# A gate projection by Strassen-Winograd's seven half-block products, beside a state space stage and a prompt attention stage

## The reference

```python
u = rms_norm(x, lp['norm_g'][0])
nq, nkv, ngate, sz, sxbc, sdt, dqkv, mg = split_in(u @ lp['w_in'])
...                                   # o_a, o_b, o_cc: the three mixers
gates = jax.nn.sigmoid(mg.reshape(B, T, 3, D_MODEL).astype(jnp.float32)).astype(x.dtype)
mix = (gates[:, :, 0] * o_a + gates[:, :, 1] * o_b + gates[:, :, 2] * o_cc) @ lp['w_out']
```

```python
cb = jnp.einsum('bcihn,bcjhn->bcijh', Cc, Bc) * decay * dtc[:, :, None]
y_diag = jnp.einsum('bcijh,bcjhp->bcihp', cb, xc)
h_last, h_in = lax.scan(step, h0.astype(f32), (jnp.moveaxis(states, 1, 0), jnp.moveaxis(chunk_decay, 1, 0)))
y_off = jnp.einsum('bcihn,bchpn,bcih->bcihp', Cc, h_in, jnp.exp(acum))
```

## Time and profile before

| | |
|---|---|
| median of 3 runs | 3345.62 us (3342.29 to 3346.05) |
| the profiled execution | 3336.09 us |
| its span in the trace | 3334.3 us |
| mean granted TensorE clock | 0.951 of full |
| PE busy | 3026.4 us (91%) |
| DVE busy | 1254.0 us (38%) |
| ACT busy | 640.2 us (19%) |
| POOL busy | 468.8 us (14%) |

### The profile page before, as it was taken

One profiled execution on the slowest core, in us unless ns is written; L12 is line 12 of the kernel. 1 busy time (PEld: TensorE's weight loads), 2 busy tenths in 40 slices (PEclk: granted clock), 3 DMA queues, 4 the chain that ended last, 5 costly groups with the idle time before them and its releaser, 6 DMA issues. The chain is left out here.

```text
span 3334.3 us, 42907 instructions
## 1 busy us (share of the span) xinstructions
PE 3026.4 (91%) x15198; PEld 2011.2 (60%) x15198; DVE 1254.0 (38%) x2964; ACT 640.2 (19%) x1528; POOL 468.8 (14%) x351
## 2 busy tenths in 40 slices
PE   7999989798998888798999889799689999998998
PEld 5777766565555555445545556355478888873443
DVE  2111123233641666154554344123355655560000
ACT  2111000001321233133333221134301111110000
POOL 0001000003310433100000000011123223320000
PEclk8999999899998889899999989799899999999999
DMA  7545252426962532621110242401033433404000
GB/s 160 132 89 98 81 151 87 132 83 178 278 198 88 169 111 63 192 70 37 31 40 33 98 153 92 174 13 38 26 134 109 150 109 118 140 24 164 33 33 25
DMA packets 336639, 344.79 MB, mean 103 GB/s; under 512 B 60945, under 2 KB 305361, under 8 KB 335078
## 3 DMA queue, kind: packets, MB, share of 16 engines
q1 hardware_dynamic: 298074, 265.85, 27.4%
q10 hardware_dynamic: 38390, 76.67, 6.8%
HBM read 289.11 MB, written 110.01 MB: 120 GB/s over the span
## 5 line engine op out<-in xcount | busy, mean ns | idle before, releaser
L284 PE MATMUL d_ps<-d_w,mixer_u_T 128*128 128x288 f32 (+2 forms) x2048 | 618.8, 442 | 22.3 <-DVE d_ob L308 15.8
L284 PEld LDWEIGHTS d_ps<-d_w,mixer_u_T 128*128 128x128 f32 x2048 | 380.3, 197 | 160.1 <-issue 45.1
L288 PE MATMUL d_ps<-mixer_u_T,d_w 128*128 128x352 f32 x1152 | 426.9, 496 | 12.3 <-PEq L145 9.7
L2883 PE MATMUL down_ps<-down_w,feed_g_T 128*128 128x512 f32 x704 | 305.2, 596 | 10.6 <-DMA down_w<-ffn_w_down 10.6
L288 PEld LDWEIGHTS d_ps<-mixer_u_T,d_w 128*128 128x128 f32 x1152 | 205.4, 198 | 118.0 <-issue 55.1
L2883 PEld LDWEIGHTS down_ps<-down_w,feed_g_T 128*128 128x128 f32 x704 | 134.5, 191 | 179.7 <-issue 168.4
L3097 PE MATMUL ffn_ps<-up_u_T,ffn_w 128*128 128x264 f32 x704 | 164.6, 393 | 0.7 <-DVE ffn_taps L3243 0.7
L308 DVE COPY d_ob<-d_ps 128x288 f32<-128x288 f32 (+3 forms) x144 | 66.3, 462 | 261.9 <-PE d_ps L284 167.8
L3097 PE MATMUL ffn_ps<-ffn_T,ffn_w 128*128 128x264 f32 x704 | 163.8, 386 | 0.0
L3097 PE MATMUL ffn_ps<-up_u_T,ffn_S 128*128 128x264 f32 x704 | 163.8, 386 | 0.0
L3097 PEld LDWEIGHTS ffn_ps<-up_u_T,ffn_w 128*128 128x128 f32 x704 | 133.4, 192 | 23.5 <-issue 0.9
(11 more groups left out here) (464 smaller groups left out, 3788.4 us busy)
## 6 DMA issues: line engine op xcount, KB each, us to landing
out_dil_sample<-cache_dil_w ACTq DMA_DIRECT2D x10, 3264.0 KB
ffn_w<-ffn_w_up SPq DMA_DIRECT2D x44, 512.0 KB, 4.9
cmp_rows<-cache_nsa_kv SPq DMA_DIRECT2D x128, 128.0 KB
graw<-d_ob SPq DMA_DIRECT2D x72, 176.0 KB
mix_gate<-graw SPq DMA_DIRECT2D x24, 528.0 KB, 6.1
dils_qb<-proj SPq DMA_DIRECT2D x24, 512.0 KB, 7.0
d_w<-w_in SPq DMA_DIRECT2D x24, 512.0 KB, 5.3
ssd_x<-proj SPq DMA_DIRECT2D x29, 384.0 KB, 4.8
```

Of the source, the lines that this page charges most:

```text
L284: mm = pe.matmul(self.ps[u % 2][0:rows, 0:cols], self.u_T[:, k, r0:r0 + rows], self.view(i)[:, k, :], start=(k == 0), stop=(k == DK - 1))
L288: mm = pe.matmul(self.ps[u % 2][:, 0:cols], self.view(i)[:, k, x, :], self.u_T[:, k, c * third:(c + 1) * third], start=(k == 0), stop=(k = ...
L2883: mm = pe.matmul(ps[i % ring][:, 512 * h:512 * (h + 1)], lhs_T[:, k, r0:r0 + m], w[:, k, 512 * h:512 * (h + 1)], start=(k == 0), stop=(k = ...
```

## The change

The gate projection leaves `Dense` for a class of its own, `Gates`. It takes the weights in pairs of blocks (A, 2 by 2 half blocks: two rows of 128 channels, two columns of 512 features) and the activations in halves (B: two of 512 features, two of 528 tokens), and computes the four half blocks of the product by seven products instead of eight. Each of the seven runs twice, for x = 0 and 1, over 264 tokens, with 4 steps: 14 products and 56 steps for a pair, 6 pairs a stage, so 336 steps and 672 PE instructions of 264 columns a stage where there were 288 and 576 of 352. P1 is copied out by ACT to `kept`; every other result is taken out of PSUM by a DVE addition with what was kept (14 of 128x264 a pair, 84 a stage; two of them behind P5). A bank is used by the products of one x in turn, so a product waits until the addition before it on that bank is done. The sums S of weights (4 a pair, 128x512) are GpSimd's, the sums T of activations are made once by DVE at the head of the `ssd` stage. The stores to `graw` become 96 of 128x264 in place of 72 of 128x352.

To make room, `oa` in `nsap` has two heads' places instead of four, so that ACT waits for a store before it writes a place again; and in `ssd` two small buffers are laid over others (`junk` over `yout`, `last_rows` over `skip`) with a wait on ACT each.

```diff
+class Gates:
+    ORDER = [(p, x) for p in ("P1", "P2", "P6", "P7", "P5", "P4", "P3") for x in range(2)]
+    OUTS = [("C11", 0), ("C11", 1), ("C22", 0), ("C22", 1), ("C21", 0), ("C21", 1), ("C12", 0), ("C12", 1)]
...
+        last_reader = dict(P6="C11", P7="U", P5="W", P4="V", P3="C21")
+        operands = dict(P1=(lambda i: self.A(i, 0, 0), lambda x: self.B(0, 0, x)),
+                        P2=(lambda i: self.A(i, 0, 1), lambda x: self.B(1, 0, x)),
+                        P6=(lambda i: self.S(2), lambda x: self.T_of(1, x)),
+                        P7=(lambda i: self.S(3), lambda x: self.B(0, 1, x)),
+                        P5=(lambda i: self.A(i, 1, 0), lambda x: self.T_of(0, x)),
+                        P4=(lambda i: self.A(i, 1, 1), lambda x: self.T_of(2, x)),
+                        P3=(lambda i: self.S(4), lambda x: self.B(1, 1, x)))
...
+                for p, x in ORDER:
+                    if p == "P2":
+                        pe.wait_ge(self.held, 2 * i + x + 1)
+                    elif p != "P1":
+                        pe.wait_ge(self.summed, self.added(i, last_reader[p], x))
+                    elif i:
+                        pe.wait_ge(self.summed, self.added(i - 1, "C12", x))
...
+                    for k in range(KH):
+                        mm = pe.matmul(self.ps[x][:, 0:self.quarter], lhs(i)[:, k, :], rhs(x)[:, k, :], start=(k == 0), stop=(k == KH - 1))
...
+                        act.copy(self.kept[:, 0, x, :], self.ps[x][:, 0:self.quarter]).then_inc(self.held, 1)
...
+            def add(i, name, x, base, out):
+                if (name, x) in OUTS:
+                    o = OUTS.index((name, x))
+                    n = len(OUTS) * i + o
+                    if n >= RING:
+                        dve.wait_ge(self.stored[o % RING], 16 * (n // RING))
+                    out = self.ob[:, o % RING, 0:self.quarter]
+                dve.tensor_tensor(out, base, self.ps[x][:, 0:self.quarter], ALU.add).then_inc(self.summed, 1)
...
+                    if p == "P2":
+                        add(i, "C11", x, first, None)
+                    elif p == "P6":
+                        add(i, "U", x, first, second)
+                    elif p == "P7":
+                        add(i, "W", x, second, first)
+                    elif p == "P5":
+                        add(i, "C22", x, first, None)
+                        add(i, "V", x, second, second)
+                    elif p == "P4":
+                        add(i, "C21", x, first, None)
+                    elif p == "P3":
+                        add(i, "C12", x, second, None)
...
+                pool.tensor_tensor(self.S(3), self.A(i, 0, 0), self.A(i, 1, 0), ALU.subtract).then_inc(self.S_made, 1)
...
+        return Lane(KH * NP * pairs, pe_program, act_program, dve_program, pool_program, sp_program)
...
-    oa = st.sb("oa", [P, NSA_R, SEQ])
+    oa = st.sb("oa", [P, 2, SEQ])
...
-            act.activation(junk[0:m, :], y[0:m, :], ACT.Square, accum_out=ss[0:m, 0:1]).then_inc(squared, 1)
+            if n >= 2:
+                act.wait_ge(stored[slot], s_count(n, slot))
+            act.activation(yout[0:m, slot, :], y[0:m, :], ACT.Square, accum_out=ss[0:m, 0:1]).then_inc(squared, 1)
...
-            ssd(nc, ins, outs, proj, y_b, ident, [(dense.lane(36, settle=False), 0, 1)])
+                ssd(nc, ins, outs, proj, y_b, ident, [(gates_of.lane(6), 0, 1)])
...
-                together(nc, (dense.lane(36), 0, 1), (nsa_prompt_lane(nc, own, ins, proj, kc_T, vc, oa_T, ident), 0.08, 0.92),
+                    together(nc, (gates_of.lane(6), 0, 1), (nsa_prompt_lane(nc, own, ins, proj, kc_T, vc, oa_T, ident), 0.08, 0.92),
```

More of the change, by code:

```diff
@@ L174, with __init__ @@
     RING = 4
[L176 to L180, removed]
+    def __init__(self, nc, st, u_T, ins, proj, parts):
+        self.u_T, self.proj, self.parts = u_T, proj, parts
+        self.w = st.sb("w", [P, 2, DK * max(n for _, n in parts)])
+        self.ob = st.sb("ob", [P, self.RING, max(n for _, n in parts)])
         self.ps = [st.ps(f"ps{i}", [P, 512]) for i in range(2)]
@@ L303, in copy_out @@
                         eng.wait_ge(self.stored[u % ring], self.stored_by(u % ring, u))
-                    narrow = self.chunk(u) and 4 * cols - parts[self.units[u][0]][2]
+                    narrow = self.chunk(u) and 4 * cols - parts[self.units[u][0]][1]
                     if narrow:
@@ L328, in sp_program @@
                     self.load(sp, i + 1)
+                elif j == 1:
+                    sp.wait_ge(self.product, self.first[i])
+                    self.behind(sp)
                 if u > lo:
@@ L748, in act_program @@
                     act.wait_ge(pv, group0[s + 1] - group0[0])
-                    act.copy(oa[:, r, i * P:(i + 1) * P], O[s % 2][:, :]).then_inc(out_made, 1)
+                    if r >= 2 and i == 0:
+                        act.wait_ge(stored, 16 * (r - 1))
+                    act.copy(oa[:, r % 2, i * P:(i + 1) * P], O[s % 2][:, :]).then_inc(out_made, 1)
                 yield
@@ L3950, in decoder_step @@
         u_T = part.sb("u_T", [P, DK, TOK])
-        parts = [("proj", C_Q + i * (C_Z // 4), C_Z // 4) for i in range(4)]
-        parts += [("proj", C_DIL + i * ((C_MG - C_DIL) // 8), (C_MG - C_DIL) // 8) for i in range(8)]
-        parts += [("proj", C_Z + i * ((C_DIL - C_Z) // 4), (C_DIL - C_Z) // 4) for i in range(4)]
-        parts += [("gate", q, P) for q in range(0, 3 * DK, 2)]
+        parts = [(C_Q + i * (C_Z // 4), C_Z // 4) for i in range(4)]
+        parts += [(C_DIL + i * ((C_MG - C_DIL) // 8), (C_MG - C_DIL) // 8) for i in range(8)]
+        parts += [(C_Z + i * ((C_DIL - C_Z) // 4), (C_DIL - C_Z) // 4) for i in range(4)]
         with Stage(nc, "d") as d_st:
-            dense = Dense(nc, d_st, u_T, ins, proj, graw, parts)
+            dense = Dense(nc, d_st, u_T, ins, proj, parts)
+            gates_of = Gates(nc, d_st, dense, ins, graw)
+            dense.behind = lambda sp: gates_of.load(sp, 0)
             with Stage(nc, "front") as own_f, Stage(nc, "cmp") as own:
@@ L3970, in decoder_step @@
                                                   (scores, 0.05, 0.66), (values, 0.3, 0.67))
[L3971 to L3975 removed]
+            with Stage(nc, "gate_sums") as own_g:
+                gates_of.open(own_g)
+                ssd(nc, ins, outs, proj, y_b, ident, [(gates_of.lane(6), 0, 1)])
+                with Stage(nc, "nsap") as own:
+                    together(nc, (gates_of.lane(6), 0, 1), (nsa_prompt_lane(nc, own, ins, proj, kc_T, vc, oa_T, ident), 0.08, 0.92),
+                             (branch_weights_lane(nc, own, proj, o_dil, lse, gates), 0.3, 0.3),
+                             (copies_lane(kept + moves, moved), 0, 1))
     with Stage(nc, "feed") as part:
```

198 lines of the change are left out of this document (154 added, 44 removed).

## The result

The changed kernel takes 3400.28 us (median of 4 runs, 3393.68 to 3401.62) against 3343.95 us before on the same chip: a ratio of 1.0166, 95% interval 1.0148 to 1.0184. It is slower by 56 us. The forecast had the sign right, and late `ssd_Y` as one place of the loss, but only 22 of the 56 us, and its range ended at 3398.

A forecast was written before the change was run, and what follows sets the result against it. PE is busiest, but a chain through DVE, ACT, DVE, PE and DVE was taken to bound `ssd` chunks. +30 in `ssd` and -8 in `nsap` on 3336.09 gave 3358, plus 9.5 to the median: 3368 us, range 3325 to 3398.

The forecast's parts named there:

- late `ssd_Y`: In `ssd` chunks, ssd_Y starts later because the PE product ahead of it waits for a DVE addition: +21 us, 10 to 32.
- +30: Sum of all terms for the `ssd` stage: +30 us, from +4 to +95.
- `nsap`, -8: `nsap` stage: -12.8 us from less PE work, +5 from additions ahead of exponentials; sum -8, from -17 to +5.
- GpSimd beside DVE, +5 in `ssd`: In `ssd`, GpSimd's 24 sums slow DVE sums running beside them: +5 us, from 0 to 30.
- before, those steps ran while PE waited anyway: In `ssd` chunks, gate steps left ahead of ssd_Y formerly filled PE's wait, now delay it; one chunk 2.5 us late.
- The additions, +4.7: In `ssd`, 17 additions in DVE's unbroken runs cost 7.3 us, less 2.6 for copies: +4.7, from 0 to 26.
- PE's work removed: Gate instructions in `ssd` and `nsap`: 173 us of PE work becomes 149.5, 23.3 us less in each stage.
- predicted 3, at its end: At the end of `ssd`, where gates are the larger part of PE's work, 13% less of them gives -3 us.
- Setup, +5: End of `ssd` setup: three DVE additions needing a store stand ahead of last states and first convolution: +5 us, 0 to 7.
- that PE falls to 1.2 GHz more often: Rival in `ssd`: more waits put a further third of PE's instructions at half rate, +25 us, 3393; chance 0.12.
- Stores held DVE: Rival: additions wait for an earlier store's buffer once a pair for 3 us, 36 us in all, 3400; chance 0.05.

The follow-up runs named there:

- copies_only: Changed kernel without sums S and T and without additions, each product copied from PSUM by ACT (x = 0) or DVE (x = 1): 3339.4 us, ratio 0.9994.
- no_s: As pool_first, with GpSimd's sums S left out and unsummed blocks multiplied in their place: 3364.9 us, ratio 1.0044.
- pool_first: Changed kernel with GpSimd's four sums for the first pair of `nsap` issued ahead of the scaling of the tables (L1005): 3381.1 us, ratio 1.0121.
- y_ahead: As pool_first, with ssd_Y on PE moved up right behind ssd_TS, ahead of the gate steps between them: 3376.2 us, ratio 1.0100.
- copies_dve: As copies_only, but all 14 results of a pair are copied by DVE, none by ACT: 3369.7 us, ratio 1.0085.
- copies_long: As copies_only, but two products in a row go into one accumulation, 8 results a pair instead of 14: 3334.8 us, ratio 0.9974.
- idle_adds: As copies_only, plus one DVE addition of 128x264 that no bank or store waits for behind each of a pair's 14 products: 3362.3 us, ratio 1.0060.

## Why the prediction was wrong

The forecast was +22 us. Two steps failed: in `ssd` the wait that was counted was too narrow (+30 for a measured 45.6), and in `nsap` GpSimd was put at nothing, which made -8 of a measured +14.4. The second is the larger part of the miss.

- **`nsap`, -8.** Wrong in sign: +14.4. From kernel to kernel, copies_only is 16.1 us under before (PE's work), no_s 0.6 over that (the additions), pool_first 11.5 over that (the sums S), and after 18.4 over that (the sums S behind L1005). The first two were forecast at -12.8 and +5, the last two not at all. The head was the failure of method: I read DVE's and PE's order but not GpSimd's in this stage, where L488 stands behind L1005.
- **GpSimd beside DVE, +5 in `ssd`.** The price was 1.8 there, not told from nothing. It was missing in `nsap`, where it is 11.5: I had looked for DVE sums of two tensors only. The rule of the Trainium skill, "SBUF — State Buffer", "Who interferes with whom", was quoted with its half on one SBUF input; the same section adds that a tensor_scalar can enter a mode that takes the shared ports. L977 is one, and the trace agrees: the six took 4.76 us beside the sums where they took 1.96.
- **Late `ssd_Y`, +21.** The observation was right, the mechanism too narrow. 21.6 us appear at just this place. y_ahead lets `ssd_Y` start at once, leaves 17.3 of the 21.6 us at L2008's place in the order, and `ssd` as long as it was. The step that failed is "before, those steps ran while PE waited anyway", with its conclusion that only the product ahead of `ssd_Y` matters: of PE's 76.7 us of waits for banks, 48.0 stand elsewhere. With both banks freed by DVE and 4 steps of slack, a long run of DVE stops PE, and a stop of PE can hold the next addition. The cost belongs to the arrangement: 29.6 us for releasing both banks through DVE (copies_dve against copies_only), 11.0 for products of half the length with their copies. The high end of this term was added up wrong as well: 19.8, 15 and 2 are 37, not 32.
- **The additions, +4.7.** "I count two a chunk, 17 in all, that stand in its unbroken runs" priced them as time of DVE. As instructions they cost nothing over copies (no_s and copies_dve, 356.0 and 355.9 us); as the release of both banks they are the largest term.
- **PE's work removed.** The pitch of the earlier trace rows held, 0.2225 us an instruction. But the sum set a duration, 10.81 / 36, against a distance between starts. By starts (36 from 1107.49 to 1118.15, where the next row begins) the old instructions take 0.296 each, so that 21.1 us a stage go, not 23.3. They are worth 16.1 us in `nsap` (predicted 12.8), and none shows in `ssd` (predicted 3, at its end; from the last chunk on the stage is 1.3 us longer than before).
- **Setup, +5.** This part grew by 7.8 us. The wait for a store, 6.26 us at 1109.06, was seen rightly, but the first convolution starts only 3.7 us later against the start of the stage; the rest comes behind, where three additions wait 4.4 us in all for products ahead of the second convolution (one copy waited 1.5 us there before).
- **The rivals.** That PE falls to 1.2 GHz more often is seen (0.87 in `ssd` where it was 0.91), but it goes with the waits: copies_only with 0.88 is 28 us shorter. Stores held DVE once, in the setup, not once a pair; that this rival's 3400 is the measured time is chance, and its own sum, 3368 and 36, gives 3404.

Open: 6.5 us of `ssd` between copies_long and before; how much of the 14.6 us of idle_adds is DVE's time and how much its place in the queue; and what the lower clock adds to each step. No run here keeps the seven products in `ssd` with additions and sums and yet wins.

## What to carry to other kernels

When a cheaper scheme turns copies into additions, as here, the engines that free a PSUM bank can go from two to one; if that engine also runs a long in-order chain beside, compare slack per bank (steps of the product before the wait) with the longest run on that engine, before counting matmuls. A stall that shows at one instruction of two coupled queues can be moved by reordering without being paid off: change what frees the resource, not the place of the wait. Read the order of every engine to which the change gives work, the least busy first: the first instruction of a stage there may wait for the last load.

## What the runs showed of the hardware

DVE operations of one SBUF tensor and one column (TENSOR_SCALAR) were held up beside GpSimd: with 31 columns 0.98 us beside a sum of 128x512 and 0.24 alone, with 512 columns 1.52 and 0.48, and one of 7 columns 3.29 us beside GpSimd's TENSOR_SCALAR of 128x1215, against 0.23 alone. DVE additions that read PSUM and one SBUF tensor kept to 406 to 431 ns in the whole run. A sum of 128x512 takes 0.685 us on DVE and 1.27 on GpSimd, and moving 24 of them onto DVE, already the busier of the two, shortened the stage by 12 us.
